# A decoder layer on one core: memory keys and values as the first stage, cross-attention tokens split unnormalised, residuals added by VectorE out of PSUM

## The reference

```
h = rmsnorm(x, norm_mix_g);  proj = h @ w_in          # attention (NSA), spatial gating, merge gates
merged = sigmoid(gA) * (o_a @ w_proj_a) + sigmoid(gB) * (o_b @ w_proj_b)
x = x + merged @ w_mix_out
hx = rmsnorm(x, norm_cross_g);  hm = rmsnorm(mem, norm_mem_g)
mq = (hx @ w_mq) * 128 ** -0.5                        # 4 heads of 128
mk, mv = split(hm @ w_mkv)                            # 256 x 512 each
p = softmax(mq @ mk.T);  x = x + (p @ mv) @ w_mo      # cross-attention, per head
hf = rmsnorm(x, norm_ffn_g);  gt, up = split(hf @ w_ffn_in)
x = x + (silu(gt) * up) @ w_ffn_out                   # hidden width 5632
return rmsnorm(x, norm_final_g)
```

## Time and profile before

| | |
|---|---|
| Time, median of three runs (lowest to highest) | 3023.8 us (3019.54 to 3024.85) |
| The profiled execution: its time, its span | 3020.6 us, 3018.9 us |
| Mean granted TensorE clock | 0.993 |
| Busy: TensorE, VectorE, ScalarE, GpSimd | 97%, 52%, 21%, 27% of the span |
| Products L549 to L551 with `act_hi`, `act_lo`: count, busy | 3 x 2832, 3334 us |
| Mean DMA traffic | 100 GB/s |
| Chain that ended last: TensorE, VectorE | 88%, 5% of the span |

### The profile page before, as it was taken

The page is one execution under the profiler, slowest core; times in us unless marked ns, Lnnn a source line. Parts: engine busy times, 40 slices in busy tenths (PEclk is TensorE's granted clock), DMA queues, the critical chain, the costliest instruction groups (busy, mean ns, idle before and its releaser), DMA issues.

```text
span 3018.9 us, 39451 instructions
## 1 busy us (share of the span) xinstructions
PE 2935.1 (97%) x13845; PEld 2433.6 (81%) x13845; DVE 1579.2 (52%) x2833; ACT 628.8 (21%) x1394; POOL 800.0 (27%) x638
## 2 busy tenths in 40 slices
PE   6999999999999999998989999999999999999997
PEld 5887888888888788887768888888888888888886
DVE  4434666666555575448584444444444444444454
ACT  3011444444212332112231111000111100011111
POOL 0100333333105553113162222111222211122232
PEclk9999999999999999999999999999999999999999
DMA  6323322223334545334123333333333333333332
GB/s 194 94 77 75 88 76 82 83 79 84 105 99 104 160 133 139 107 101 126 56 84 97 97 94 94 94 95 96 97 97 97 97 98 97 97 97 97 89 105 99
DMA packets 543164, 300.56 MB, mean 100 GB/s; under 512 B 9076, under 2 KB 533480, under 8 KB 541672
## 3 DMA queue, kind: packets, MB, share of 16 engines
q1 hardware_dynamic: 532768, 285.63, 34.3%
q10 hardware_dynamic: 10312, 13.83, 1.4%
HBM read 286.84 MB, written 12.58 MB: 99 GB/s over the span
## 4 chain that ended last, share of the span: by engine, by line
PE 88%; DVE 5%; DMA 2%; POOL 2%; issue 1%; ACT 1%; ACTq 0%; SPq 0%; DVEq 0%; POOLq 0%
PE bank L549 28%; PE bank L551 27%; PE bank L550 27%; DVE w_lo L929 1%; PE bank L715 1%; DVE w_hi L927 1%; PE bank L685 1%; DMA rows_bc<-in_sgu_b_dram 1%; PE bank L700 1%; DVE act_lo L1164 1%; DVE bank L1028 1%; PE bank L613 0%; PE bank L795 0%; DVE prob_t L1047 0%; PE bank L680 0%
## 5 line engine op out<-in xcount | busy, mean ns | idle before, releaser
L549 PE MATMUL bank<-act_hi,w_hi 128*128 128x512 f32 x2832 | 1123.1, 397 | 7.2 <-DVE act_lo L1164 4.0
L551 PE MATMUL bank<-act_hi,w_lo 128*128 128x512 f32 x2832 | 1105.8, 390 | 0.0
L550 PE MATMUL bank<-act_lo,w_hi 128*128 128x512 f32 x2832 | 1105.5, 390 | 0.0
L927 DVE CAST w_hi<-raw 128x512 fp32r<-128x512 f32 (+1 forms) x996 | 493.7, 496 | 1161.1 <-PE bank L551 1135.0
L929 DVE TENSOR_TENSOR w_lo<-raw,w_hi 128x512 fp32r<-128x512 f32 (+1 forms) x996 | 788.3, 791 | 34.3
L551 PEld LDWEIGHTS bank<-act_hi,w_lo 128*128 128x128 f32 x2832 | 531.4, 188 | 114.5
L549 PEld LDWEIGHTS bank<-act_hi,w_hi 128*128 128x128 f32 x2832 | 532.0, 188 | 109.0 <-DVE act_lo L1164 5.1
L550 PEld LDWEIGHTS bank<-act_lo,w_hi 128*128 128x128 f32 x2832 | 532.5, 188 | 98.1 <-issue 0.2
L549 PE MATMUL bank<-ff_hi,w_hi 128*128 128x512 f32 x704 | 275.3, 391 | 0.0
L551 PE MATMUL bank<-ff_hi,w_lo 128*128 128x512 f32 x704 | 274.1, 389 | 0.0
L550 PE MATMUL bank<-ff_lo,w_hi 128*128 128x512 f32 x704 | 274.0, 389 | 0.0
(11 more groups left out here) (231 smaller groups left out, 2693.1 us busy)
## 6 DMA issues: line engine op xcount, KB each, us to landing
raw<-in_w_ffn_in_dram SPq DMA_DIRECT2D x88, 1024.0 KB, 5.6
raw<-in_w_in_dram SPq DMA_DIRECT2D x68, 1024.0 KB, 5.7
raw<-in_w_ffn_out_dram SPq DMA_DIRECT2D x32, 1024.0 KB, 5.8
raw<-in_w_mix_out_dram SPq DMA_DIRECT2D x16, 1024.0 KB, 6.1
raw<-in_w_ffn_out_dram SPq DMA_DIRECT2D x16, 768.0 KB, 5.0
merge_gates<-gate_out ACTq DMA_DIRECT2D x32, 256.0 KB, 2.0
raw<-in_w_proj_a_dram SPq DMA_DIRECT2D x16, 512.0 KB, 4.3
raw<-in_w_proj_b_dram SPq DMA_DIRECT2D x16, 512.0 KB, 5.5
```

The costliest lines, as they stand in the source:

```text
L549: pe.matmul(dst, w_hi[:, q, j, 0:m], hi, start=first, stop=False)
L550: pe.matmul(dst, w_hi[:, q, j, 0:m], lo, start=False, stop=False)
L551: return pe.matmul(dst, w_lo[:, q, j, 0:m], hi, start=False, stop=last)
L927: dve.tensor_copy(w_hi[:, q, :, 0:width], src).then_inc(hi_done, 1)
```

## The change

Keys and values of mem are computed first, in the new phase order mk, mv, c, q, ... While they are, x is squared, scaled, turned and split in between (`X_AT` says at which panel and quarter), and in this stage ScalarE makes the high parts of the weights (`high`) and VectorE the low parts only (`low`). Keys and values are stored to DRAM and loaded again (`mem_back`) when wo has ended. In wo the residual products are gone: TensorE transposes x's columns into a bank of their own, ScalarE moves them to `xt`, and VectorE adds the group's PSUM bank to `xt` (`add_x`). The tokens of the cross-attention get their gain but not their rms; both parts are made in wo, and `rms_bc` is multiplied in when VectorE takes the queries out of PSUM. `xg`, the GpSimd low parts and `NORMED_AT` go. Products of the first four w_mo tiles are put into steps 16, 17, 20, 21 and 22 of mq, as soon as their heads are ready. In mo VectorE adds the bank to `xt`, ScalarE makes the high parts of the weights, and GpSimd keeps the sum of squares only. Buffers get other places. The loops of wo and mo are unrolled.

```diff
-        ("c", (4,)), ("q", (8,)), ("k", (4,)), ("v", (4,)), ("g", (1,)), ("merge", (32,)),
-        ("sv", (8,)), ("su", (8,)), ("ab", (16, 4, 2, 2)), ("wo", (16,)), ("mk", (4,)), ("mv", (4,)),
+        ("mk", (4,)), ("mv", (4,)), ("c", (4,)), ("q", (8,)), ("k", (4,)), ("v", (4,)), ("g", (1,)),
+        ("merge", (32,)), ("sv", (8,)), ("su", (8,)), ("ab", (16, 4, 2, 2)), ("wo", (16,)),
...
+        MO_BANKS = (PH["mo"].group0 % 2, (PH["mo"].group0 + 1) % 2, 6, 2)
+        X_SLOTS = [(p, q) for p in range(4, 8) for q in range(4)][2:]
+        X_AT = {pq: [k] for k, pq in enumerate(X_SLOTS)}
+        X_AT[7, 2], X_AT[7, 3] = [12, 13], [14, 15]
...
@@ sync
-            for c in range(0, TC, 2):
-                sp.dma_start(x_rows[:, c], x_v[:, c]).then_inc(x_landed[c], 16)
+            for c in range(MC):
+                sp.dma_start(mem_rows[:, c], mem[0].rearrange("(c p) n -> p c n", p=P)[:, c]).then_inc(mem_landed[c], 16)
+            columns(PH["mk"], mkv_v, 0, peel=True)
+            columns(PH["mv"], mkv_v, 512)
...
+            for n in range(2):
+                panel(ph, *ph.at(n), [(0, 16, mq_v[:, :, n * P:(n + 1) * P])])
+            sp.wait_ge(mem_kept, 32)
+            sp.wait_ge(quarters_done, PH["wo"].end())
+            sp.dma_start(mk_t[:].rearrange("p h m -> p (h m)"), mk_dram).then_inc(mem_back, 16)
+            sp.dma_start(mv_rows[:].rearrange("p c f -> p (c f)"), mv_dram).then_inc(mem_back, 16)
...
@@ tensor
+            for k in range(4):
+                turn_mem(k)
             pe.wait_ge(cols_ready, 1)
+            for p in range(8):
+                ph, i, u = kv_panel(p)
+                wait(pe, banks_read, p - 1)
+                for q in range(4):
+                    if p == 0:
+                        for k in range(4 * q + 4, min(4 * q + 8, DK)):
+                            turn_mem(k)
+                        pe.wait_ge(mem_lo, 4 * q + 4)
+                    quarter(ph, i, u, q, bank[p % 2][:, 0:MEM], lambda k: hm_hi[:, k], lambda k: hm_lo[:, k], q == 0, q == 3, 4 * q)
+                    if q == 1 and p > 4:
+                        turn_mem_values(p - 5)
+                    for k in X_AT.get((p, q), ()):
+                        turn_x(k)
...
-                    def residual(dst):
-                        pe.wait_ge(xcol_landed[u], i * 16 + 16)
-                        for c in range(TC):
-                            pe.matmul(dst[:, c * P:(c + 1) * P], x_cols[:, u, c], ident[:], start=False, stop=False)
...
+                    for c in range(TC):
+                        mm = pe.transpose(bank[2 + u][:, c * P:(c + 1) * P], x_cols[:, u, c], ident[:])
+                    mm.then_inc(x_turned, 1)
+                    group(ph, i, u, hi16, lo16, ready=(merge_lo_done, 0) if isinstance(i, int) and u == 0 else None)
...
+                    if step == 1:
+                        norm_total(sumsq, DK)
+                elif step < 18:
+                    n = step - 16
+                    pe.wait_ge(banks_read, ph.group0 + 3 + n)
+                    pe.wait_ge(mo_lo_done, 2)
+                    pe.wait_ge(split_done, PH["mo"].quarter(0, 0) + n + 1)
+                    for h in range(2):
+                        out_tile(n, h)
+                elif step == 20:
+                    pe.wait_ge(mo_lo_done, 3)
+                    for n in range(2):
+                        out_tile(n, 2)
+                elif step in (21, 22):
...
+                    for h in range(3):
+                        out_tile(n, h)
...
@@ vector
+            def low(ph, i, u, q):
+                n = ph.quarter(i, u) + q
+                s = ph.slot(u)
+                dve.wait_ge(hi_done, n + 1)
+                dve.tensor_tensor(w_lo[:, q], raw[:, s, 4 * q:4 * q + 4], w_hi[:, q].bitcast(F32), ALU.subtract).then_inc(split_done, 1)
...
+                if step == 2:
+                    inverse(0, rms_bc)
+                if step in (4, 8, 12, 16):
...
+                    dve.scalar_tensor_tensor(out=mq_t[:, h], in0=bank[(ph.group0 + h) % 2][:], scalar=P ** -0.5, in1=rms_bc[:],
+                                             op0=ALU.mult, op1=ALU.mult).then_inc(banks_read, 1)
...
+            for n in range(DK):
+                dve.wait_ge(quarters_done, ph.quarter0 + n + 1)
+                dve.tensor_tensor(xt[:, n], xt[:, n], bank[MO_BANKS[n] if n < 4 else (ph.group0 + n) % 2][:], ALU.add).then_inc(banks_read, 1)
+                p, q = divmod(n + 4, 4)
+                if p < 4:
+                    low(ph, *ph.at(p), q)
+                else:
+                    low(PH["f0"], 0, 0, q)
+                if n > 0:
+                    gained_low(n - 1, G_FFN, DK)
...
@@ scalar
+            act.wait_ge(cols_turned, 1)
+            act.activation(cols[:], bank[0][:, 0:116], ACT.Copy).then_inc(cols_ready, 1)
+            act.wait_ge(ones_made, 2)
+            act.wait_ge(mem_landed[1], 16)
+            act.activation(junk[:, 0], mem_rows[:, 1], ACT.Square, accum_out=ss[:, 1:2]).then_inc(mem_sq, 1)
+            for c in range(TC):
+                act.dma_start(x_rows[:, c], x_v[:, c]).then_inc(x_landed[c], 16)
...
+            for p in range(8):
+                for q in range(4):
+                    high(*kv_panel(p), q)
+                    if p == 0:
+                        for k in range(4 * q, 4 * q + 4):
+                            mem_high(k)
+                    if (p, q) == (1, 1):
+                        x_square(0)
+                    if (p, q) == (2, 1):
+                        x_square(2)
...
@@ gpsimd
-            for k in range(DK):
-                split_lo(k, 0)
...
-                        pool.tensor_tensor(xt[:, ds(n, 1), :], xt[:, ds(n, 1), :], add_in[:, j % 2], ALU.add).then_inc(added, 1)
...
+            for n in range(DK):
+                total(sumsq, mo_sq[:, n % 2], n + DK)
```

482 lines of the change are left out of this document (239 added, 243 removed).

## The result

The changed kernel takes **2970.0 us** (median of 4 runs, 2968.91 to 2971.25), the kernel before 3022.4 (4 runs, 3019.54 to 3024.85): a ratio of 0.9827, 95% interval 0.9810 to 0.9844. The forecast was 2974, 2960 to 2992. The profiled execution took 2968.91 us with a span of 2967.2, where the earlier trace rows has 3018.9 around it: 51.7 us less. TensorE is now at 98%, and all engines do a little less.

What follows compares the result with a forecast made beforehand. TensorE, busy 97% of the span, was taken as the bound. Gains of 21.8 + 11.5 + 16.3 = 49.6 us bring the profiled 3020.6 to 2971; with 3.2 for the median the forecast is 2974, range 2960 to 2992.

Steps and rivals of the forecast that it cites:

- Part A: Start and keys and values, now computed first: 99.85 us before, 78 after, a gain of 21.8.
- The squares' 3 us: Keys-and-values panels 1 to 3: squaring x in the same in-order queues adds 3 us to 17.3 of products.
- Rival 2: First stage short of lead: later start, full-length squares and scaling, slower panel 0; 15.7 us lost, 2990; 14%.
- Rival 3: First stage: the clock stays low because handshakes leave TensorE idle in each quarter; 3016; 4%.
- Rival 4: First stage bound by loads: at 22 us per load a panel takes 13.6, total 3037; 3%.
- Gated feed-forward ... 0: Gated feed-forward, 1450 us: other addresses but the same instructions, so a gain of 0.
- Part B: w_mix_out: residual products and mem transposes go, x transposes come; 0.75 us less a panel, 11.5 taken as gain.
- The lower bound, 5: w_mix_out: gain of only 5 us if x's transposes are as slow as its first turns, 0.18 each.
- Part C: Queries to the first f0 panel: 144.7 us before, 128.4 after, a gain of 16.3, by the tail's bounds 12 to 20.
- the far bound: Attention tail: 24.9 us if the 36 w_mo products put there fill none of its idle time.
- the near end: w_mo: VectorE needs 2.1 us a tile, not 3.1, as GpSimd's sum starts when VectorE's SBUF operations are mostly through.
- Rival 1: w_mo stays VectorE-bound: every tile pays a full collision, 3.3 us, 53 us where the forecast has 41; 2986; 12%.

Runs made afterwards that it cites:

- experiment 3: Changed kernel, first stage varied: x's 16 turns in one lump 2972.2 us; squares of x left out 2968.7; mem squared earlier and x's squares later 2971.5.
- experiment 1: Kernel before with mem's 2 MB load and ScalarE's squares of it two pairs of panels later in the ab stage: 3017.0 us against 3020.1.
- experiment 2: Kernel before without the eight residual products a panel in w_mix_out: 3002.3 us against 3020.1, ratio 0.9942.
- pool_none: Changed kernel with GpSimd's sum of squares left out in the w_mo stage: 2969.7 us, ratio 0.9834 to the kernel before.

## Why the prediction was right or wrong

**The bound.** Right. TensorE sets the time, and the ledger's gains are idle time of TensorE, time at its lower clock, or instructions of its own that went. The 3.2 us that the forecast adds from the profiled execution to the median were 1.1.

**Part A, 19.6 for 21.8.** The steps hold to within 2 us each. (The bounds named there, a start at 14 or at 24.32, give 13 to 23.5, not 12 to 26.) The first transposes of mem came at 17.44, not 15.7: mem landed early enough (its first half was squared from 6.44 on), but ScalarE's copy of the small vectors stands ahead of its Square, and those landed at 10.89. Yet panel 1 began at 27.58 (27.7 forecast), and panel 4 at 48.3 (48). The rest is in panels 4 to 7: a turn is 0.43, not 0.36 (1.1 over 16), and a wait of 1.07 at 51.08 stands behind ScalarE's scaling of x, for which 0.6 was allowed. The squares' 3 us were 2.2. Rival 2, the short lead, names the right place and sizes it far too high. Rival 3 is refuted, but not by the row that I set against it: the clock was low at the start, in both kernels. TensorE's first transposes came 0.21 us apart, up to 28.62 us before and 21.38 after, and 0.11 apart behind that in the kernel before (experiment 3); the 1.00 of the earlier trace rows for 24.32 to 37.37 is, in its first 4.3 us, time without a record. So the trace bears out what rival 3 quotes, a low level first, and my sentence against it was a misreading. What the rival needs beyond that, a low level that lasts through the panels, didn't come: products are 0.12 us apart from 21.44 on. Rival 4 is refuted too: with x's 4 MB beside them, w_mkv's loads took 6.1 us at the median.

**Between parts A and B, 8.0 for 0.** This is one of the two steps that failed. "Gated feed-forward ... 0" was right, but no line of the sum asked what removing the mem load from the ab stage would give there. The trace of before held it all: the load, the weight load beside it, TensorE's 3.61. The prediction counted mem's DMA where it arrives and not where it had left. 5.1 us are shown by experiment 1. 2.4 are a stretch at the lower clock that the changed kernel happened not to have in this execution and one of its variants had in full: luck. The other 0.5 is how the stretches were cut.

**Part B, 10.8 for 11.5.** The panels came 11.36 us apart (181.81/16), 11.3 forecast. The earlier trace rows was the right row, and the residual's own price is confirmed by experiment 2. A turn is 0.42 there, not 0.28. The lower bound, 5, took 0.18 a transpose as a wait for VectorE; it was the lower clock.

**Part C, 13.1 for 16.3.** This is the other step that failed: the tail, where I had the overlap wrong. Up to it 56.26 (0.5 + 55.2 forecast). The tail took 25.98; I had 20.9 (the middle of the bounds 17.4 and 24.9 is 21.15). The forecast's 16.6 is counted from the first score, and counted so the tail is 25.4, still beyond the far bound. Two things were not in that bound. The tail without any fill was not 16.6 but 17.8, since VectorE scaled the last queries behind a weight split, and the score that waits for them came 2.2 us later behind the one before it (4.88 us for 2.68). And the far bound had the fills at worst add their own time; 12 of them cost nothing, but the 24 behind the last score cost their own 5.5 and more, with the wait for mo_lo, which was named and not priced, and the lower clock behind it (1.6 by pool_none). What follows was better than forecast: w_mo's rest 38.49 against 35.9 + 3.3 + 1.5, tile 4's wait 1.89, and no clock drop behind it, which again is luck, as pool_none has one there. The f0 panel 10.87 for 11.1.

**VectorE's tile.** The condition held: VectorE kept TensorE's pace, 2.75 us a tile from the fifth add to the last, though for four tiles it was 2.9. My range was 2.1 to 3.1, and I took the near end. My reason, that GpSimd starts when VectorE's two SBUF operations are mostly through, is what the kernel without fills shows. With the change's fills it doesn't hold, and the two operations take 1211 and 1068 ns for 693 and 787. Rival 1 at 3.3 a tile didn't come; with a second GpSimd operation it was 3.15. The Trainium skill (GPSIMD Engine Reference, Specifications) has GpSimd contend with VectorE's instructions that have two SBUF inputs or a two-port mode, which an add with one input in PSUM is not; by this rule, the traces agree: 676 to 688 ns for the add in every variant, 691 to 1714 for the two with both inputs in SBUF.

## What to carry to other kernels

When a load moves, look at both ends: what it delayed where it was may be worth more than what it costs where it goes. Work put into idle time must fit into the pause where it stands: six products in front of a score that waited 3.63 us anyway were free, and so were lots of three in the pause for a copy, while lots of six and nine in front of transposes whose pauses are 0.5 to 1.4 us cost their full length. Before pricing two engines' collision, see whether the slowed one has a pause to give: here VectorE's SBUF operations took half as long again, and TensorE hardly noticed. And check a granted clock of 1.00 at the start of a trace against the distances of equal instructions.

## What was unexpected of the hardware

- TensorE began at its lower clock level in both kernels: its first 128x128 transposes came 0.21 us apart, and 0.11 from 28.62 us on in the kernel before, while the profile's clock column says 1.00 for both.
- A 3.61 us wait of TensorE was followed by 3 us of products every 0.43 us instead of 0.23 (granted clock 0.72 over 6 us). The 1.73 us wait in the tail was followed by 3.4 us at 0.50 in the changed kernel, and by none in pool_none with the same instructions; tile 4's wait of 1.9 us by no loss in the first and by 0.68 over 4 us in the second. The waits of 1.54 and 0.42 us in attention were followed by 0.51 over 6.1 us in the kernel before and in one variant of the changed kernel, and by 1.00 in the changed kernel.
- While mem's 2 MB landed at 347 GB/s in all, a 512 KB weight load issued beside it was usable 12.3 us later (this load is 5.5 at the median of 16); with mem out of the way VectorE had the same weights 5.3 us earlier (cast at 1004.26 instead of 1009.57).
